# Mixer projections as products of high and low parts, their weights fetched in two pieces, the remainders made on GpSimd

## The reference, cut to what matters

```python
def hybrid_mixer(x, cos, sin, w_in, b_gate, ...):
    proj = x @ w_in
    (dq, dk, dv, dz, da, dbeta, glu, c_q, c_kv, k_r, gate_logits) = jnp.split(proj, _split_points(), axis=-1)
    y_dn = deltanet_branch(dq, dk, dv, dz, da, dbeta, ...)
    y_cv = conv_branch(glu, ...)
    y_mla = mla_branch(c_q, c_kv, k_r, ...)
    gates = jax.nn.sigmoid(gate_logits + b_gate).reshape(b, t, N_BRANCHES, d)
    merged = gates[:, :, 0] * y_dn + gates[:, :, 1] * y_cv + gates[:, :, 2] * y_mla
    return merged @ w_out
```

## Time and profile before

| | us |
|---|---|
| three runs: lowest, median, highest | 3149.6, 3158.2, 3164.7 |
| the profiled execution | 3149.6 |
| its span, first to last instruction | 3147.8 |
| PE busy in it | 2997.1 |
| DVE, ACT, POOL busy | 1887.3, 1364.4, 46.9 |

### The profile page before, as it was taken

The page is one execution under the profiler, slowest core; times in us unless marked ns, Lnnn a source line. Parts: engine busy times, 40 slices in busy tenths (PEclk is TensorE's granted clock), DMA queues, the critical chain, the costliest instruction groups (busy, mean ns, idle before and its releaser), DMA issues.

```text
span 3147.8 us, 42901 instructions
## 1 busy us (share of the span) xinstructions
PE 2997.1 (95%) x16078; PEld 2469.9 (78%) x16078; DVE 1887.3 (60%) x2391; ACT 1364.4 (43%) x1562; POOL 46.9 (1%) x93
## 2 busy tenths in 40 slices
PE   8999999999999999889999999988999999999998
PEld 7997886599899878767988699454877887788776
DVE  6755632377677464326670454153887788778876
ACT  4431321144444122213531244132676667666765
POOL 2000010000000000000000000000000000000000
PEclk9999999999899999999999999998999999999999
DMA  8753321387577433126753365323999999999995
GB/s 285 240 180 138 134 81 55 107 267 243 195 260 241 146 117 107 56 80 228 253 187 107 134 199 169 117 76 109 358 328 320 341 338 328 320 340 339 328 321 211
DMA packets 375931, 659.69 MB, mean 210 GB/s; under 512 B 11626, under 2 KB 197848, under 8 KB 375832
## 3 DMA queue, kind: packets, MB, share of 16 engines
q1 hardware_dynamic: 375832, 658.32, 60.3%
HBM read 657.23 MB, written 1.05 MB: 209 GB/s over the span
## 4 chain that ended last, share of the span: by engine, by line
PE 76%; DVE 8%; issue 6%; ACT 4%; PEld 2%; DVEq 2%; DMA 1%; PEldq 1%; ACTq 1%; SPq 0%
PE banks L669 16%; PE banks L670 15%; PE banks L671 15%; PE banks L1143 9%; PE banks L1961 3%; PE banks L1993 3%; PE banks L1327 2%; PE banks L665 2%; DVE expert_rest L1069 2%; PE banks L742 1%; DVE ffn_arena L1008 1%; PE banks L1208 1%; PE banks L829 1%; DVE mod_sum L1001 1%; PE banks L841 1%
## 5 line engine op out<-in xcount | busy, mean ns | idle before, releaser
L669 PE MATMUL banks<-ffn_arena 128*128 128x256 f32 (+1 forms) x3460 | 1169.1, 338 | 46.2 <-DVE ffn_arena L1029 14.0
L671 PE MATMUL banks<-ffn_arena 128*128 128x256 f32 (+1 forms) x3460 | 1149.8, 332 | 0.0
L669 PEld LDWEIGHTS banks<-ffn_arena 128*128 128x128 f32 x3460 | 661.8, 191 | 123.8 <-issue 38.7
L1069 DVE TENSOR_TENSOR expert_rest<-expert_raw,ffn_arena 128x2048 fp32r<-128x2048 f32 (+1 forms) x306 | 646.2, 2160 | 118.5 <-ACT ffn_arena L928 117.4
L671 PEld LDWEIGHTS banks<-ffn_arena 128*128 128x128 f32 x3460 | 661.7, 191 | 69.1
L670 PE MATMUL banks<-ffn_arena 128*128 128x256 f32 (+1 forms) x2200 | 673.7, 306 | 0.0
L928 ACT ACTIVATE ffn_arena<-expert_raw 128x2048 fp32r<-128x2048 f32 (+1 forms) x306 | 538.6, 1815 | 113.7 <-PE banks L671 111.7
L670 PE MATMUL banks<-expert_rest,ffn_arena 128*128 128x512 f32 (+1 forms) x1224 | 465.9, 381 | 0.0
L670 PEld LDWEIGHTS banks<-ffn_arena 128*128 128x128 f32 x2200 | 424.7, 193 | 17.5 <-issue 0.5
L1143 PE MATMUL banks<-HT,panel 128*128 128x256 f32 x1280 | 281.1, 380 | 2.5 <-issue 2.5
L1143 PEld LDWEIGHTS banks<-HT,panel 128*128 128x128 f32 x1280 | 242.2, 190 | 37.5 <-issue 5.3
(11 more groups left out here) (401 smaller groups left out, 2777.9 us busy)
## 6 DMA issues: line engine op xcount, KB each, us to landing
expert_raw<-in_moe_w_gate_dram SPq DMA_DIRECT2D x90, 1024.0 KB, 5.2
expert_raw<-in_moe_w_up_dram SPq DMA_DIRECT2D x90, 1024.0 KB, 5.4
expert_raw<-in_moe_w_down_dram SPq DMA_DIRECT2D x90, 1024.0 KB, 5.1
gate_w<-in_ffn_w_gate_dram SPq DMA_DIRECT2D x55, 1024.0 KB, 5.4
up_w<-in_ffn_w_up_dram SPq DMA_DIRECT2D x55, 1024.0 KB, 5.4
down_w<-in_ffn_w_down_dram SPq DMA_DIRECT2D x55, 1024.0 KB, 5.4
mod_unit<-in_mod_w_dram SPq DMA_DIRECT2D x48, 1024.0 KB, 5.2
panel<-in_w_in_dram SPq DMA_DIRECT2D x24, 2048.0 KB, 7.8
```

The source lines that it names most:

```text
L669: mm(out, w[0], x[0], start=start, stop=False)
L671: return mm(out, w[1], x[0], start=False, stop=stop)
L1069: tt(rest[:, half, :], tile[:, half, :], high[:, half, :].bitcast(F32), ALU.subtract).then_inc(expert_lo, 1 if h else 1 + skipped)
```

## The change

Uses 1 to 4, 5, 6 and 8 to 13 (`SPLIT_USES`) become three fp32r products. Each is cut into two halves, 24 in a layer, numbered q = 0 to 23 (0 to 7 are uses 1 to 4, 8 and 9 `z`, 10 and 11 `lora`, 12 to 23 the gates). A half is 1 MB of weights and 2048 words in each partition: 256 of the columns, or for `z` and `lora` 4 of the 8 row blocks. SP fetches each half by itself; in a run of column uses half h of use u waits only for half h of use u - 2. ACT copies the half to fp32r (`high`) into one of three slots in the unused buffers of the feed forward's weights (`mix_high`). POOL subtracts and writes the remainder over the raw half (`mix_low_pool`). PE waits for it (`half_low`) and runs 48 matmuls of 256 columns, or 24 of 512 for a half of `z` or `lora`. x gets its two parts at the start of the mixer, one copy on ACT and one subtraction on DVE. Since those lie where gates 8 to 23 would go, gates 8 to 15 go to `HT`, and the last four pairs of gates are taken after the last projection, one in each of rounds 1 to 4. Use 0, use 7, the 8 columns of a and beta and everything from use 14 on stay in float32. The fetches of the second feed forward wait for the last projection. The rest of the diff moves semaphore counts.

```diff
@@ -93,6 +93,11 @@
 assert len(MIXER_PANELS) == MIX_USES
+COLUMN_USES, ROW_USES = (1, 2, 3, 4, 8, 9, 10, 11, 12, 13), (5, 6)
+SPLIT_USES = sorted(COLUMN_USES + ROW_USES)
+MIX_HALVES = 2 * len(SPLIT_USES)
+MIX_SPLITS = MIX_HALVES + 1
+SECOND_LAYER = 16 * len(SPLIT_USES) // 2
 
@@ -416,6 +428,14 @@
             return E_BASE + expert_done(i, name, before) * 2 - 1 + h
+
+        def mix_half(q):
+
+            use, h = SPLIT_USES[q // 2], q % 2
+            if use in ROW_USES:
+                cols = 520 if use == 5 else PANEL
+                return [v3(t[use % 2], 0, KD, cols)[:, 4 * h:4 * h + 4, 0:512] for t in (panel, panel_rest)] + [v3(mix_high, q % 3 * 2048, 4, 512)]
+            return [v3(t[use % 2], 0, KD, PANEL)[:, :, h * SEQ:(h + 1) * SEQ] for t in (panel, panel_rest)] + [v3(mix_high, q % 3 * 2048, KD, SEQ)]
 
@@ -492,6 +512,18 @@
 
+            def split_load(pieces, use, l):
+                name, r0, nr, c0, cols = pieces[0]
+                src = a[name][bass.ds(l, 1), r0:r0 + nr, c0:c0 + cols].rearrange("o (k p) n -> p (o k) n", p=P)
+                dst = v3(panel[use % 2], 0, KD, cols)
+                for h, landed_half in enumerate((panel_in, panel_in_second)):
+                    if use in COLUMN_USES and use - 2 in COLUMN_USES:
+                        sp.wait_ge(pair_done, l * 22 + (2 * (use - 2) + h + 1 if use < 8 else 2 * (use - 2) + h - 5))
+                    else:
+                        sp.wait_ge(panel_used, l * MIX_USES + use + 1)
+                    part_of = (lambda t: t[:, 4 * h:4 * h + 4, :]) if use in ROW_USES else (lambda t: t[:, :, h * SEQ:(h + 1) * SEQ])
+                    sp.dma_start(part_of(dst), part_of(src)).then_inc(landed_half[use % 2], 16)
+
             def norm_loads(which, l):
@@ -536,9 +568,13 @@
-                    panel_load(pieces, l * MIX_USES + use, use % 2, l)
+                    if use in SPLIT_USES:
+                        split_load(pieces, use, l)
+                    else:
+                        panel_load(pieces, l * MIX_USES + use, use % 2, l)
                     if use == 4:
                         norm_loads("ln2", l)
+                sp.wait_ge(pair_done, l * 22 + 22)
                 ffn_loads(of_layer("ffn2_w_gate", l), of_layer("ffn2_w_up", l), of_layer("ffn2_w_down", l), n + NS,
@@ -635,19 +671,30 @@
 
+            def mix_low_pool(l, q):
+                raw_, rest, high = mix_half(q)
+                pool.wait_ge(half_high, l * MIX_SPLITS + q + 2)
+                nc.gpsimd.tensor_tensor(rest, raw_, high.bitcast(F32), ALU.subtract).then_inc(half_low, 1)
+
             with pool.Fori(0, DEPTH) as l:
 
+                for q in range(12):
+                    mix_low_pool(l, q)
                 pool.wait_ge(z_taken, l + 1)
                 z = z_tok.rearrange("p t (h v) -> p (t h) v", h=HEADS)
                 nc.gpsimd.tensor_tensor(z, z, norm_row[:].rearrange("p (o v) -> p o v", o=1).to_broadcast([P, TT * HEADS, HD]),
                                         ALU.mult).then_inc(z_scaled, 1)
 
+                for q in range(12, 22):
+                    mix_low_pool(l, q)
                 pool.wait_ge(lower_ready, l + 1)
                 for i in range(1, 6):
                     if i > 1:
                         pool.wait_ge(turn_done, l * 10 + 2 * (i - 1))
                     nc.gpsimd.tensor_tensor(part.rearrange("p t h c -> p (t h) c"), lower.rearrange("p t h c -> p (t h) c"),
                                             level[:, i:i + 1, :].to_broadcast([P, TT * HEADS, P]), ALU.mult).then_inc(part_ready, 1)
+                    if i < 3:
+                        mix_low_pool(l, 21 + i)
 
@@ -1137,18 +1184,18 @@
 
-            def project(tile, c, bank, half):
-
-                for k in range(KD):
-                    last = mm(bank[:, half * SEQ:(half + 1) * SEQ], tile[:, k, c:c + P], HT[:, k, :], start=k == 0, stop=k == KD - 1)
-                return last
+            def half_ready(q):
+                pe.wait_ge(half_low, l * MIX_HALVES + q + 1)
+                return mix_half(q)[:0:-1]
 
             def projection(use, first_pair):
-                tile = v3(panel_ready(use), 0, KD, PANEL)
                 for j in range(2):
+                    weights = half_ready(2 * SPLIT_USES.index(use) + j)
                     bank = pair_bank(first_pair + j)
                     for half in range(2):
-                        last = project(tile, (2 * j + half) * P, bank, half)
+                        for k in range(KD):
+                            last = split_mm(bank[:, half * SEQ:(half + 1) * SEQ], [w[:, k, half * P:(half + 1) * P] for w in weights],
+                                            [v[:, k, :] for v in x_parts], k == 0, k == KD - 1)
                     last.then_inc(pair_done, 1)
@@ -1185,27 +1232,33 @@
+            pe.wait_ge(mix_low, l + 1)
             for use in range(1, 3):
                 projection(use, 2 * use)
             for use in range(2):
                 projection(3 + use, 6 + 2 * use)
 
+            def row_halves(use, bank):
+                for h in range(2):
+                    weights = half_ready(2 * SPLIT_USES.index(use) + h)
+                    for t in range(TT):
+                        for j in range(4):
+                            k = 4 * h + j
+                            last = split_mm(banks[:, bank + t, :], [v[:, k, t * P:(t + 1) * P] for v in x_parts],
+                                            [w[:, j, :] for w in weights], k == 0, k == KD - 1)
+                    last.then_inc(half_used, 1)
+
+            small_bank = pair_bank(10)
+            row_halves(5, 0)
+            pe.drain().then_inc(z_done, 1)
             tile = v3(panel_ready(5), 0, KD, 520)
-            small_bank = pair_bank(10)
-            for t in range(TT):
-                for k in range(KD):
-                    last = mm(banks[:, t, :], HT[:, k, t * P:(t + 1) * P], tile[:, k, 0:512], start=k == 0, stop=k == KD - 1)
-            last.then_inc(z_done, 1)
             for t in range(TT):
@@ -1473,20 +1526,40 @@
 
+            def high(q):
+                use, h = SPLIT_USES[q // 2], q % 2
+                if h == 0:
+                    act.wait_ge(panel_in[use % 2], l * LANDED_LAYER[use % 2] + landed(use))
+                else:
+                    act.wait_ge(panel_in_second[use % 2], l * SECOND_LAYER + 16 * (sum(u % 2 == use % 2 for u in SPLIT_USES[:q // 2]) + 1))
+                if 11 <= q < 15:
+                    act.wait_ge(half_used, l * 4 + q - 10)
+                elif q > 2:
+                    act.wait_ge(pair_done, l * 22 + (q if q < 11 else q - 4))
+                raw_, _, dst = mix_half(q)
+                copy(dst, raw_).then_inc(half_high, 1)
+
             def gate_pair(i):
-                act.wait_ge(pair_done, l * 22 + i)
+                act.wait_ge(pair_done, l * 22 + (i if i < 19 else 22))
                 for half in range(2):
                     b = 2 * (i - 11) + half
-                    last = act_fn(gates[:, b, :], banks[:, 4 + i % 4, half * SEQ:(half + 1) * SEQ], ACT.Sigmoid,
+                    dst = HT[:, b - KD, :] if KD <= b < 2 * KD else gates[:, b, :]
+                    last = act_fn(dst, banks[:, 4 + i % 4, half * SEQ:(half + 1) * SEQ], ACT.Sigmoid,
                                   bias=pcol[:, ROW_GATE + b:ROW_GATE + b + 1])
                 last.then_inc(pair_taken, 1)
 
+            act.drain()
+            copy(x_parts[0], HT[:]).then_inc(half_high, 1)
+            high(0)
+            high(1)
             act.wait_ge(rope_ready, 2 * l + 1)
             act_fn(sine.rearrange("p s t c -> p (s t c)"), arena[:, 0:P], ACT.Sin)
             act_fn(cosine.rearrange("p s t c -> p (s t c)"), arena[:, P:2 * P], ACT.Sin)
             for i in range(6):
                 act.wait_ge(pair_done, l * 22 + i + 1)
                 copy(raw[:, 2 * i:2 * i + 2, 4:260], banks[:, 4 + i % 4, :].rearrange("p (a b) -> p a b", a=2)).then_inc(pair_taken, 1)
+                if i:
+                    high(i + 1)
             act.drain()
@@ -1496,6 +1569,8 @@
                 last.then_inc(pair_taken, 1)
+                high(i + 1)
+            high(11)
             act.wait_ge(qkv_conv, l + 1)
@@ -1511,11 +1586,13 @@
             mod_act(act, l * 2, banks[:, 5, 0:16])
+            high(12)
 
             act.wait_ge(tok_done, l + 1)
             for i in range(4):
                 last = act_fn(qk_sq[:, i, :, :].rearrange("p h c -> p (h c)"), banks[:, i, :], ACT.Square)
             last.then_inc(tok_sq, 1)
+            high(13)
 
@@ -1525,8 +1602,11 @@
             act_fn(tok_sum, tok_sum, ACT.Sqrt, bias=L2_EPS).then_inc(tok_std, 1)
+            high(14)
             gate_pair(11)
+            high(15)
             gate_pair(12)
+            high(16)
             act.wait_ge(v_done, l + 1)
@@ -1536,7 +1616,9 @@
             gate_pair(13)
+            high(17)
             gate_pair(14)
+            high(18)
             act.wait_ge(back_done, l * 2 + 2)
@@ -1564,9 +1647,10 @@
```

(38 more changed lines are left out.)

## The result

The changed kernel takes 3195.3 us (median of 4 runs, 3192.1 to 3204.1) for 3154.9 us of the kernel before (4 runs): a ratio of 1.0129, 95% interval 1.0108 to 1.015. That is 1.3% slower; the forecast was 1.7%. The profiled execution spans 3190.3 us at a mean granted clock of 0.964; before it was 3147.8 us at 0.981.

What follows compares the result with a forecast made beforehand. PE bounds the kernel; its saving of 61 us is outweighed by remainders on POOL that hold DVE. Sum: 27 us a layer slower, 54 in all, 3204 profiled, 3212 us median, 1.7% slower; range 3150 to 3255.

Steps and rivals of the forecast that it cites:

- PE's own saving: Split projections: a column use takes 11.86 us instead of 14.41; 30.5 us a layer, 61 in all, if all else is hidden.
- rival 1: Remainders hardly hold DVE, under 3.0 us lost by each; PE's saving stays, 23 us a layer, 3112 us; chance 0.13.
- its own case: Case 4: POOL's remainders hold DVE, which delays PE; 27 us a layer slower, 3180 to 3245 us; chance 0.74.
- The price of a remainder: POOL's subtraction of 2048 words takes 4.7 us, twice the 2.35 us of 1024 words.
- What DVE loses by one: POOL and DVE operations on two SBUF operands exclude each other; DVE loses a remainder's whole time, 4.7 us.
- Three of its signs: Signs of a right forecast: taps 0 to 19 over 50 us, decay tables over 25 late, PE idle 20 before v.
- The start: Mixer's start: POOL's first remainders hold DVE's angles until about 236.5; remainder 2 ends at 246.2, PE waits 4 us.
- The chain behind tap 19: From tap 19 until q and k are scaled: 0.7 us for `soft_ready` and 9.0 us from the first table load.
- Behind the first round: Solve: rounds 1 and 2 contain uses 12 and 13 and get 5.1 us shorter; then nothing changes.
- rival 3: POOL's remainder itself is the bound: over 5.8 us PE waits for every half; 3360 us at 9.4; chance 0.04.
- Rival 2: It comes out even: DVE loses 2.5 to 3.5 us a remainder or gets in more often; 3142 to 3174; chance 0.09.
- The point of no gain: At under 3.0 us lost by DVE to a remainder, the changed kernel is no longer slower.

Runs made afterwards that it cites:

- e1_short: Changed kernel with POOL subtracting 128 words of most remainders instead of 2048, PE's third product reusing the high weights: 3120.1 us, ratio 0.9885.
- e5_dve2: e3_dve in a second order: more taps in DVE's idle time, remainder 19 and copy 12 moved ahead: 3112.0 us, ratio 0.986.
- e3_dve: Changed kernel with all remainders on DVE instead of POOL, placed by hand, and the taps spread out: 3125.5 us, ratio 0.9918.
- e6_dve2_fill: e5_dve2 with eleven more filler matmuls a layer in PE's short waits behind the solve: 3121.7 us, ratio 0.988.

## Why the prediction was right, point by point

It named the mechanism and the sign, and the size within its range. Its sum was 27 us a layer and 54 in all; measured were 20.8 at the end of the first (the transposes of H that follow it, 641.66 for 620.89) and 42.5 in all. 2.7 of the 20.8 came behind the solve, where the forecast had nothing change. Times of the first layer, in us:

| step | before | forecast | measured |
|---|---|---|---|
| half 2 starts | | 246.2 | 244.8 |
| DVE's convolution starts | 259.8 | 258.4 | 257.0 |
| taps 0 to 19 done | 326.6 | 355.9 | 348.9 |
| v turned | 350.45 | 365.6 | 357.8 |
| taps 20 to 27 done | 367.9 | 404.1 | 394.2 |
| DVE's clamp done | 375.5 | 408.8 | 398.7 |
| first round of the solve | 405.0 | 435.2 | 425.6 |
| end of the solve | 461.8 | 486.8 | 479.9 |

- *PE's own saving*: the pace is right. Two neighbouring matmuls of a half start 0.12 us apart, two halves of e1_short take 11.87 us with their gap (232.23 to 244.10) for my 11.86, and the mixer saves 22.7 us once nobody makes PE wait, for the 23 of rival 1. That match is partly luck: the 23 held 4 us for a wait that e1_short does not have, and e1_short has others (use 1 starts at 232.23 for 230.63, and PE waits 1.3, 0.7 and 2.9 us for DVE and ACT up to the first round). Two things were not in the sum. One is the part that a lower clock takes back elsewhere. The other is the wait for remainder 12, 3.4 us, which the prediction had priced under rival 1 and left out of its own case: use 8 ended at 341.0, not at about 337. It cost nothing, because PE was ahead of DVE there.
- *The price of a remainder*: right. 4.77 us for 4.7.
- *What DVE loses by one*: the mis-sized term. The sum took the whole of POOL's time. From 256.97 to 302.10, from 303.57 to 348.93 and from 367.45 to 394.17 POOL was busy for 29.6, 11.7 and 13.8 us, 55.1 together. DVE's same work took 27.1, 8.9 and 12.8 us longer than in the earlier trace rows, 48.8 together. But in the earlier trace rows the tap beside the gains had itself lost 1.9 us, so beside an idle POOL the work would have been 50.7 us shorter: 0.92 of POOL's time, or 4.4 us a remainder. The rest is, as I read it, time in which DVE was between two operations, or finished one that had begun first. Up to tap 19 it makes 92.0 us instead of 97.5, 5.5 of the 7.8 us by which v was turned earlier than forecast. Of these 5.5, 3.0 are the share of 0.92, 0.6 are remainders that were a little shorter, and 1.9 are an error in the sum: its 36.5 us for taps 0 to 19 already held the 1.9 lost beside the gains, and it added the gains' 2.4 once more.
- *A near miss that is partly luck*: the prediction gave 3196 us for a loss of 4.2 us a remainder, and 3195.3 was measured. The loss was 4.4; the double count, the start, the shorter chain behind tap 19, what did not come back in the rounds and the clock make up the rest, in both directions.
- *Three of its signs were set too high*: taps 0 to 19 lie over 45 us (not over 50), the clamp is 23 us late (not 25), and PE stands 16.7 us before it turns v (the sign was 20 or more, the sum about 28), 7.8 of it because v came earlier and 4.0 because use 8 ended later.
- *The start*: 1.4 us too pessimistic. DVE's angles were held as said, and ended at 236.7, the estimate 236.5.
- *The chain behind tap 19*: 8.8 us instead of 9.7. ACT had loaded its sigmoid's table before it began to wait, at 328.05.
- *Behind the first round*: 5.1 us were to come back. In e1_short they do (387.31 to 439.12 is 51.8 for 56.8); in the changed kernel 2.5 come back; the granted clock is 0.50, its lower level, from 424 to 430, after the stall of PE before the first round, and the first round's 16 matmuls take 3.75 us for 2.02.

Rival 1 (the remainders hardly hold DVE) and rival 3 (POOL itself the bound) fall by the longest tap and by the 4.77 us. Rival 2, even, is what 1536 words give, and its condition, a loss of 2.5 to 3.5 us, is met there. The point of no gain, 3.0 us lost by a remainder, was a straight line through a curve that bends: it lies at an estimated 3.4. The Trainium skill (SBUF — State Buffer, section "SBUF: two separate sides") says that the one that starts first holds the pair of ports for the whole instruction, and that operations in a 2-port mode are held too, with one SBUF input. The trace agrees with both, though it does not show an operation's mode. The four L1726 have one SBUF input; they took 0.67 us before and 9.33 beside two remainders. The copy L1802 took 2.06 us beside POOL, and 0.69 in e5_dve2 without it.

## What to carry to other kernels

An idle engine is not free: before work goes to GpSimd, look at what DVE does at the same time, and count GpSimd's whole duration against DVE's operations on SBUF. Here a remainder costs DVE 2.3 us if DVE makes it itself and 4.4 us if GpSimd does. Where the bound engine is made faster, the one that came next must be scheduled anew as well: spreading the taps gave 33 us, the other engine then 33, and a second round of moves 18.

## What the runs showed of the hardware that was not expected

- DVE's operations with one input in PSUM and one in SBUF were not held. L1836 (one input in PSUM, one in SBUF) did 8 operations in 2.15 us, at 411.18, while POOL ran three remainders without a break from 406.03 to 421.24; the like 8 take 2.16 us in e3_dve, where POOL does nothing then.
- A held operation waits out POOL's, even a small one: four of 32 columns took 9.33 us beside two remainders of 9.36 us together.
- A kernel that is faster in work can be granted less clock: mean granted clock 0.981 before, 0.971 in e1_short, 0.977 in e5_dve2, in profiled executions of 3147.8, 3121.0 and 3106.2 us. Within one kernel the shorter executions are those with the higher clock (e6_dve2_fill: 3109.3 us at 0.979, 3123.8 us at 0.972).
